# Gate spreading: VectorE multiplies the gates of 4 of 16 groups, ScalarE of the other 12

## The reference

```python
eid = jnp.take_along_axis(cand_id, top_pos, axis=-1)      # first key * 128 + second key
gate = jax.nn.softmax(top_s, axis=-1)
...
hid = jnp.einsum('td,ted->te', xb, u_tab[eb])
return jnp.einsum('te,ted->td', jax.nn.gelu(hid) * gb, v_tab[eb])
```

## Time and profile before

| | |
|---|---|
| median of 3 runs | 2623.84 us (2623.11 to 2629.01) |
| profiled execution | 2628.26 us, of which the profile's span 2626.3 us |
| gate spreading in the span | 1026.5 us to 1315 us, 9 steps, a step every 31.6 us |
| busy share of the span | PE 93%, PEld 91%, DVE 58%, ACT 36%, POOL 24% |

### The profile page before, as it was taken

One profiled execution on the slowest core, in us unless ns is written; L12 is line 12 of the kernel. 1 busy time (PEld: TensorE's weight loads), 2 busy tenths in 40 slices (PEclk: granted clock), 3 DMA queues, 4 the chain that ended last, 5 costly groups with the idle time before them and its releaser, 6 DMA issues. The chain is left out here.

```text
span 2626.3 us, 50323 instructions
## 1 busy us (share of the span) xinstructions
PE 2450.3 (93%) x20078; PEld 2387.2 (91%) x20078; DVE 1523.4 (58%) x2792; ACT 950.8 (36%) x1802; POOL 642.7 (24%) x314
## 2 busy tenths in 40 slices
PE   7986888878999998999989999999999999999997
PEld 6985777778999998888889999999999999999997
DVE  4344455532698985877745445445545545777774
ACT  4234334322333335888732222223223222222221
POOL 2433244422345543111131122112112210000000
PEclk9997788859999999999989999999999999999999
DMA  4321000012233332666662323233233232455451
GB/s 177 122 102 55 26 26 14 2 67 85 83 108 105 108 116 82 189 187 191 196 219 91 103 104 112 101 110 116 92 109 106 103 104 93 170 172 177 167 177 41
DMA packets 162461, 296.02 MB, mean 113 GB/s; under 512 B 11873, under 2 KB 99233, under 8 KB 158121
## 3 DMA queue, kind: packets, MB, share of 16 engines
q1 hardware_dynamic: 162344, 294.38, 33.7%
HBM read 230.03 MB, written 64.31 MB: 112 GB/s over the span
## 5 line engine op out<-in xcount | busy, mean ns | idle before, releaser
L123 PE MATMUL banks<-w_high,v_low 128*128 128x288 f32 x2048 | 604.3, 295 | 0.0
L121 PE MATMUL banks<-w_high,v_high 128*128 128x288 f32 x2048 | 603.7, 295 | 0.4
L122 PE MATMUL banks<-w_low,v_high 128*128 128x288 f32 x2048 | 603.0, 294 | 0.0
L121 PE MATMUL banks<-res_hi,u_high 128*128 128x288 f32 x1440 | 428.0, 297 | 11.0 <-ACTq L2097 11.0
L123 PE MATMUL banks<-res_hi,u_low 128*128 128x288 f32 x1440 | 425.3, 295 | 0.0
L122 PE MATMUL banks<-res_lo,u_high 128*128 128x288 f32 x1440 | 425.0, 295 | 0.0
L121 PEld LDWEIGHTS banks<-w_high,v_high 128*128 128x128 f32 x2048 | 384.1, 188 | 3.7 <-DVE w_low L2067 3.7
L123 PEld LDWEIGHTS banks<-w_high,v_low 128*128 128x128 f32 x2048 | 384.2, 188 | 0.0
L122 PEld LDWEIGHTS banks<-w_low,v_high 128*128 128x128 f32 x2048 | 384.1, 188 | 0.0
L2091 DVE TENSOR_TENSOR res_x<-banks,res_x 128x288 f32<-128x288 f32 x512 | 225.3, 455 | 267.0 <-PE banks L123 267.0
L1713 POOL TENSOR_TENSOR u_low<-u_raw,u_high 128x1024 fp32r<-128x1024 f32 x72 | 183.8, 2554 | 705.7 <-ACT u_high L1709 705.7
(11 more groups left out here) (338 smaller groups left out, 4339.0 us busy)
## 6 DMA issues: line engine op xcount, KB each, us to landing
v_raw<-arg_v SPq DMA_DIRECT2D x128, 512.0 KB, 3.8
scratch_gates<-gate_stage SPq DMA_DIRECT2D x18, 2048.0 KB, 9.3
u_raw<-arg_u SPq DMA_DIRECT2D x36, 1024.0 KB, 6.2
gates_in<-scratch_gates SPq DMA_DIRECT2D x32, 1152.0 KB, 7.1
q_raw<-arg_u SPq DMA_DIRECT2D x38, 512.0 KB, 3.6
scratch_hidden<-gelu_ahead SPq DMA_DIRECT2D x56, 288.0 KB, 2.4
gelu_out<-scratch_hidden SPq DMA_DIRECT2D x56, 288.0 KB, 2.9
in_raw<-arg_w_in SPq DMA_DIRECT2D x25, 512.0 KB, 3.8
```

Of the source, the lines that this page charges most:

```text
L121: pe.matmul(out, ah, bh, start=first, stop=False)
L122: pe.matmul(out, ah, bl, start=False, stop=False)
L123: return pe.matmul(out, al, bh, start=False, stop=last)
```

## The change

`BY_DVE` names 4 of the 16 groups of a step: g1, g5, g10, g14. In these VectorE's comparison writes all 8 blocks (1024 columns), VectorE waits for its own comparison, and one further VectorE instruction multiplies the four second-key blocks (512 columns) in place by the gates, broadcast. ScalarE's `gate` is left out for them, and TensorE doesn't wait for `gated` there. `gated` then counts 12 a step in place of 16.

```diff
+        BY_DVE = (1, 5, 10, 14)
+        BY_ACT = [g for g in range(PER) if g not in BY_DVE]
+        NA = len(BY_ACT)
...
                         pe.wait_ge(lasts, it * PER + g + 2)
-                        pe.wait_ge(gated, it * PER + g + 2)
+                        if g in BY_ACT:
+                            pe.wait_ge(gated, it * NA + (BY_ACT.index(g) + 2))
                         pe.wait_ge(staged, it * PER + g + 1)
...
                     for g in range(LEAD):
-                        gate(it, g)
+                        if g in BY_ACT:
+                            gate(it, g)
                     for g in range(PER):
                         b, r = g // 8, g % 8
-                        if g + LEAD < PER:
+                        if g + LEAD in BY_ACT:
                             gate(it, g + LEAD)
...
-                    dve.wait_ge(gated, it * PER + 1)
+                    dve.wait_ge(gated, it * NA + 1)
...
                         dve.wait_ge(bank_done, it * PER + g + 1)
-                        n = FOUR + ACT_T
+                        n = FOUR + (ACT_T if g in BY_ACT else FOUR)
                         dve.tensor_tensor(pair[:, g % SLOTS, 0:n, :], bc(iota[:, :], 1, [P, n, N_KEYS]),
                                           bc(cur[:, g].rearrange("p a t -> p (a t)")[:, 0:n], 2, [P, n, N_KEYS]),
                                           ALU.is_equal).then_inc(onehots, 1)
-                        dve.tensor_scalar(pair[:, g % SLOTS, n, :], iota[:, :], cur[:, g, 1, ACT_T:FOUR],
-                                          curg[:, g, ACT_T:FOUR], ALU.is_equal, ALU.mult).then_inc(lasts, 1)
+                        if g in BY_ACT:
+                            dve.tensor_scalar(pair[:, g % SLOTS, n, :], iota[:, :], cur[:, g, 1, ACT_T:FOUR],
+                                              curg[:, g, ACT_T:FOUR], ALU.is_equal, ALU.mult).then_inc(lasts, 1)
+                        else:
+                            dve.wait_ge(onehots, it * PER + g + 1)
+                            o = pair[:, g % SLOTS, FOUR:, :]
+                            dve.tensor_tensor(o, o, bc(curg[:, g], 2, [P, FOUR, N_KEYS]), ALU.mult).then_inc(lasts, 1)
```

## The result

The changed kernel takes 2625.41 us (median of 20 runs, 2621.13 to 2640.57), the kernel before 2618.12 us (median of 20, 2609.07 to 2629.01, with the three runs shown ahead of the prediction among them). The ratio is 1.0038, 95% interval 1.002 to 1.0056: slower, by 5 to 15 us, where 9.7 us (1.0037) was forecast. The forecast time, 2633.5 us, lies 8 us above the measured one, and 5.7 of that is the kernel before, whose median was 2623.84 us in the three runs that the forecast started from.

A forecast was written before the change was run, and what follows sets the result against it. No engine was taken as full in the phase, so event order and the port shared by VectorE and GpSimd decide. 8 x 1.03 + 1.5 = +9.7 us on 2623.84 gave 2633.5 us, range 2622 to 2639.

The forecast's parts named there:

- the lock: VectorE's two-input instructions and GpSimd's SBUF reads exclude each other; g6's comparison would be held to 3.2 us.
- Rival 2: At g6's comparison the port costs VectorE's two-input instructions nothing: 1.08 us long, -0.67 us a step, 2618 us; chance 0.13.
- The chain of the step: From g5's multiplication through held comparisons and GpSimd's subtractions to g8, starting at 1139.54 for 1138.51: +1.03 us a step.
- the stops at g7 and g8: TensorE waits 0.94 us ahead of g7 and 0.7 ahead of g8, losing the 0.57 gained at g5.
- the wait ahead of g0: TensorE's stop at a step's start, 1.72 us, claimed to stay unchanged.
- The first step: ScalarE waits for each comparison and g5's own multiplication is held: +1.5 us taken, bounds +0.5 and +2.
- the seven steps: Steps after the first, each put at +1.03 us; the sum counted eight such steps.
- The last step: Given no term of its own; counted among the eight steps of +1.03 us.
- Rival 1: g6's comparison gets the port ahead of GpSimd's first subtraction: +0.5 us a step, 2628 us; chance 0.14.
- Rival 3: GpSimd's request falls between g5's comparison and multiplication in every step: +1.5 to 2 us a step, 2638 to 2641; chance 0.11.

The follow-up runs named there:

- e3: Changed kernel with GpSimd's subtraction cut to 128 of 1024 columns from the second step on: step 30.59 us, phase 282.6 us.
- e8: Kernel before, with TensorE's wait for `gated` put last of its three waits in a group: step 31.60 us, phase 288.9 us.
- e12: Kernel before with 13 idle semaphore increments more in TensorE's stream behind the phase: step 31.60 us, stretch behind the phase 1313.06 us.
- e1: Changed kernel with `BY_DVE` cut to g5 alone: step 32.50 us, ratio to the kernel before 1.0041.
- e5: Kernel before, with ScalarE's first rounding of u moved to its wait for the last block of the step ahead: step 30.45 us, ratio 0.9967.
- e6: Changed kernel, with ScalarE's first rounding of u moved to its wait for the last block of the step ahead: step 31.67 us, ratio 1.0013.
- e9: Kernel before with 12 empty instructions meant for TensorE's stream; they are not in the built program, so it was the kernel before again: step 31.60 us.
- e11: Kernel before with both the early first rounding of u and TensorE's wait for `gated` put last: step 30.55 us, ratio 0.9982.

## Why the prediction held

- **What bounds it, and the lock.** Shown. The port shared by VectorE and GpSimd holds two-input instructions too, in this phase and with broadcast operands (3.25 us in place of 1.08), and e3 takes the whole loss away with it. Rival 2 is out. The rule of the Trainium skill that the prediction named ("SBUF — State Buffer", section "Who interferes with whom") agrees with it, and decided the sign.
- **The chain of the step.** Each part of it is in the trace: multiplication 0.69 (0.68 forecast), subtraction 2.22 after its end (2.21), comparison 0.95 after that, tensor-scalar 2.43, the stops at g7 and g8 0.93 and 0.75 (0.94 and 0.7, from start to start). Moved onto the times of the rows, by ScalarE's first multiplication of the step (1110.83 for 1124.63), g8 starts at 1139.38 where 1139.54 was forecast and 1138.51 had been. The step costs +0.89 in place of +1.03. The 0.15 is g0, which starts so much earlier (1125.74 on that scale, against 1125.90): "the twelve register instructions more in TensorE's stream stand under its matmuls" was said, and that the wait ahead of g0 is unchanged; it was 1.56 in place of 1.72 (e8 on why).
- **The first step** took 32.11 in place of 30.12, +1.99, at the upper bound of +0.5 to +2 and 0.5 above the value taken; g5's own multiplication was held there (2.85 us), as forecast. The last step, from its copy of keys to the next phase, took 38.26 in place of 37.49, +0.77. With seven steps of +0.90 in between this is the +9.05, against 9.7 forecast: the first step was put 0.5 too low, the seven steps 0.9 too high and the last one 0.3 too high, so two errors partly cancel.
- **What was missed.** +2.5 us behind the phase, 2.0 of it from more instructions in TensorE's stream (e12). No term had it. It brings the profiles' sum to +11.5, in the upper half of the measured interval. That the forecast of 9.7 lies on the ratio's centre is therefore partly luck: the interval is 9 us wide, and the profiles say +9.05 for what was forecast and +2.5 for what was not.
- **Rival 1** was priced wrongly: when g6's comparison gets the port first, the step costs +0.90 (e1, where g5 alone is VectorE's), not +0.5, since the second subtraction then holds g7's. **Rival 3** is right for the first step, and only there.

## What to carry to other kernels

Before work moves onto VectorE, look at what GpSimd does at that moment and at which VectorE instruction would be queued behind it: two holds of some 2 us cost 0.19 us a step while they fell on instructions that nobody soon waited for, and 1.90 when they came ahead of comparisons that ScalarE needs. The share of busy time says nothing on it (VectorE rose from 24.5 to 27.5 us in 31, GpSimd has 5). And what gained was another move: taking the rounding of u out of ScalarE's way, to where ScalarE waits anyway, saved 8.5 us in the phase (e5), where giving ScalarE's multiplications to VectorE cost 9. The lock was the smaller part of that gain.

## What the runs showed of the hardware that was not expected

- Thirteen semaphore increments that nobody waits for made the stretch behind them 2.0 us longer (e12): the branch at a loop's entry took 4.03 us on TensorE in place of 0.32. So it is in all seven kernels with 11 to 14 instructions more, and in none of the five without. What happens inside stays open: in the changed kernel the branch runs from 1342.14 to 1346.11, and a 16 KB packet of instructions from 1343.60 to 1344.58, which ends 1.5 us before the branch does, so the stop does not end with it, as the expectations of e9 and e12 have it. The kernel before has such a packet too, 1.4 us after the branch begins, and does not stop.
- How soon TensorE starts after the semaphore it waits for depends on what stands between the wait and the matmul: g0 started 0.24 to 0.29 us after ScalarE's multiplication with a register instruction in between, 0.13 to 0.14 with none.
- When VectorE and GpSimd both wait for the port, GpSimd got it where it asked 0.15 us before VectorE's instruction was issued (changed kernel), 0.09 (e6) and 0.04 (the changed kernel's second subtraction of the first step, 1020.69 against 1020.73). Within 0.03 the kernel before shows both: GpSimd lost to a comparison issued 0.01 us after it, behind a running tensor-scalar, and beat a tensor-scalar issued 0.03 after it, behind a running comparison; in e11 it beat one issued 0.02 ahead of it (1102.46 against 1102.48). No run has VectorE's instruction issued clearly first while both waited: the 0.17 us of e1 is not such a case, as the comparison was running when GpSimd asked.
